# Two transformer layers on one NeuronCore: three of the memory's tiles are split into free columns beside the last projection

## Chip, cores and metric

The kernel runs on one core of a Trainium2 chip (trn2). The metric is the device time in microseconds (us) of one launch, the median of the runs shown. The engines are PE (TensorE), DVE (VectorE), ACT (ScalarE) and POOL (GpSimd). SP (SyncE) issues the transfers of the weights.

## The reference, cut to what matters

`reference()` is one hybrid layer (attention, a state-space mixer, a recurrent mixer, a feed-forward part), and then two layers of a second kind. Sequence 512, width 1024, fp32. Each of the two layers does:

```python
for l in range(2):
    y = swiglu_2(rms_norm(x, ffn1_pre_g[l]), ...);      x = x + 0.5 * rms_norm(y, ffn1_post_g[l])
    y = hybrid_mixer(rms_norm(x, mix_pre_g[l]), w_in[l], ...);  x = x + rms_norm(y, mix_post_g[l])
    y = memory_xattn(rms_norm(x, xa_pre_g[l]), rms_norm(mem, xa_mem_g[l]), wq, wk, wv, wo)
    x = x + rms_norm(y, xa_post_g[l])
    y = swiglu_2(rms_norm(x, ffn2_pre_g[l]), ...);      x = x + 0.5 * rms_norm(y, ffn2_post_g[l])

def memory_xattn(h, m, wq, wk, wv, wo):      # m: 256 x 1024
    q, k, v = h @ wq, m @ wk, m @ wv         # keys and values of the memory
    ...                                      # softmax attention of 4 heads of 256, then @ wo
```

`hybrid_mixer` projects its input to queries, keys and values of a sparse attention (96 units of scores, softmax and values here), and to the queries, keys, values and gate of a retention. The memory's keys and values do not depend on `x`, so the kernel makes them inside the mixer (class `MixerTwo`).

## The kernel before, in words

**Precision.** Every large product is made of three fp32r matmuls: high x high, high x low, low x high (`mm3`, L265). So each operand is split in two: ACT makes the high part (an activation that writes fp32r), DVE or POOL makes the low part (value minus high part). Weights come in chunks of two halves (128x1024 each): SP loads a half into one of four `raw` slots once the low part of the half before in that slot is made (`weight_load`, L231), ACT makes its high part (`weight_hi`, L238), POOL its low part (`weight_lo`, L250), in the mixer in four pieces. ACT and POOL work two chunks ahead of PE.

**The mixer's middle** is written as parallel streams, one for each engine. `Attention.pe` (L1323) runs 98 steps. In step s PE does the scores of units s and s+1 (even steps only), the transposes of unit s-1 (they wait for ACT's exp of it), the values product of unit s-2 (it waits for ACT's copy), and then takes two items ("beats") of a filler. DVE in step s adds the distances to the scores and takes the maximum (L1401, L1405), ACT takes the exp (L1373) and copies the transposes (L1382), and each then takes two beats of its own filler. So beat n belongs to step n // 2 on every engine. After each six units DVE finishes a group (L2704 to L2709), which waits for the group's last values product. Units of a group alternate between two compressed ones (32 keys) and four wide ones (384 keys in steps 48 to 71, 512 after).

**PE's filler** (`pe_filler`, L2545), one beat being six matmuls of 256 columns or three of 512: four chunks `rch` (64 beats), `vrch` and `grch` (two chunks of 16 beats each; `grch` is the last projection, the retention's gate, beats 96 to 127), three empty beats (128 to 130), the first chunk of the memory's keys `mkch[0]` (beats 131 to 138, `pe_first_keys`, one tile of the memory a beat for both column groups), `mkch[1:]` (24 beats), and four chunks of values `mvch` (32 beats, to beat 194). All of these chunks from `rch` on use PSUM banks 6 and 7, in turn. A chunk's group waits until the last reader of its bank is done (`ch.free`): for `mkch[0]` these are the gate's last two reads by DVE (L1486, `gr_used[6]` and `gr_used[7]`; each multiplies what ACT's tanh, L1475, left in `tmp` by the bank), for `mkch[1]` they are the evacuations of `mkch[0]` by DVE (L2796, `mk_kept[0]` and `mk_kept[1]`).

**The memory's split.** `self.mem` (8 tiles of 256 columns) lies in the columns where the memory's values will stand. Its split goes to `xa_mhi` and `xa_mlo`, which take the place of the mixer's input (`hhi`, `hlo`). That input is read by `grch` to its end, so ACT waits for the last matmul of `grch` (L2670) and then makes one tile a beat (L2672, beats 128 to 135; at tiles 3 and 5 it also makes a half of the weights of `mkch[1]`). DVE makes the low parts one beat later each (L2788, beats 129 to 136), waits two beats, and evacuates `mkch[0]` in beat 139. ACT has the silu's last tanh in beat 128 as well, and DVE the product after it: their generators give their four beats first and do the work at the start of the next one.

**Other streams beside the filler** are the squares of the memory, three norms, and the retention (from beat 98, every fourth beat; `Retention`, L2844), in each engine. They count the same beats, whatever the filler does in them. After the attention's last step PE begins the mixer's output projection: the half of chunk c0 that needs the retention only (`pe_out_half`, 24 matmuls of 512 columns), then the same half of c1. The weights of c1 are split after the attention on ACT and POOL: ACT waits for DVE's last group, squares (L2653), and then makes them (`weight_hi`, L2623).

Of the kernel before, what the change touches and what calls it, by code (L numbers as in the profile page):

```python
# [6 lines left out]
F32 = mybir.dt.float32  # L7
F32R = mybir.dt.float32r
ACT = mybir.ActivationFunctionType
ALU = mybir.AluOpType  # L10
AX_X = mybir.AxisListType.X

P = 128
# [251 lines left out]
def mm3(k, out, l, r, start, stop):  # L265
    t = k.nc.tensor
    t.matmul(out, l[0], r[0], start=start, stop=False)  # L267
    t.matmul(out, l[0], r[1], start=False, stop=False)  # L268
    return t.matmul(out, l[1], r[0], start=False, stop=stop)  # L269
# [26 lines left out]
def pe_stationary(k, ch, part, nk, k0=0, ktot=None, width=T, ready=None):  # L296


    t, ktot = k.nc.tensor, ktot or nk
    for m, b in enumerate(ch.banks):  # L300
        if ch.free[m] is not None:
            t.wait_ge(*ch.free[m])
        for kk in range(nk):
            if m == 0:
                pe_half_begin(k, ch, kk)
                if ready is not None:
                    for mark in ready(k0 + kk):
                        t.wait_ge(*mark)
            last = mm3(k, k.bank[b][:, 0:width], ch.weights(kk, m * P, P), part(k0 + kk), k0 + kk == 0, k0 + kk == ktot - 1)
            pe_step_end(ch, last, kk, kk == nk - 1, m == len(ch.banks) - 1)  # L310
            if width == T or kk % 2:
                yield
# [64 lines left out]
def beats(n):  # L377
    for _ in range(n):
        yield
# [25 lines left out]
class SquaresOfX:  # L405
# [9 lines left out]
    def tile(self, n):  # L415
        return self.place[:, n * T:(n + 1) * T]
# [1091 lines left out]
def idle_act(k, ch, steps):  # L1508
    yield from beats(steps)
    weight_hi(k, ch.c + 2)  # L1510
# [825 lines left out]
class MixerTwo:  # L2336
# [4 lines left out]
    def __init__(self, k, l, h):  # L2341
# [77 lines left out]

        self.mhi, self.mlo = alias("xa_mhi", k.at_h, F32R), alias("xa_mlo", k.at_h + 4 * T * 4, F32R)  # L2420
        self.m_hi, self.m_lo = k.marks("mem_hi", KT), k.marks("mem_lo", KT)
        self.mk_kept, self.mv_kept = k.marks("mem_keys", 8), k.marks("mem_values", 8)
        self.mkch = [Chunk(k, [6, 7], [self.mk_kept[2 * c], self.mk_kept[2 * c + 1]]) for c in range(4)]
        self.mvch = [Chunk(k, [6, 7], [self.mv_kept[2 * c], self.mv_kept[2 * c + 1]]) for c in range(4)]
# [120 lines left out]
    def pe_filler(self, h, part):  # L2545
        k = self.k
        for ch in self.rch:
            yield from pe_stationary(k, ch, part, KT)
        for ch in self.vrch + self.grch:
            yield from pe_moving(k, ch, h, 0, 256)  # L2550
        yield from beats(3)
        m = [self.mhi, self.mlo]
        tile = lambda n: [a[:, n * MEM:(n + 1) * MEM] for a in m]
        yield from self.pe_first_keys(self.mkch[0], tile)
        for ch in self.mkch[1:]:
            yield from pe_stationary(k, ch, tile, KT, width=MEM)
        for ch in self.mvch:
            yield from pe_moving(k, ch, m, 0, 256, width=MEM)

    def pe_first_keys(self, ch, tile):  # L2560

        k, t = self.k, self.k.nc.tensor
        for kk in range(KT):
            pe_half_begin(k, ch, kk)
            t.wait_ge(*self.m_lo[kk])
            for m, b in enumerate(ch.banks):
                if kk == 0 and ch.free[m] is not None:
                    t.wait_ge(*ch.free[m])
                last = mm3(k, k.bank[b][:, 0:MEM], ch.weights(kk, m * P, P), tile(kk), kk == 0, kk == KT - 1)
                pe_step_end(ch, last, kk, kk == KT - 1, m == 1)  # L2570
            yield

# [89 lines left out]
    def act_filler(self):  # L2662
        k, a = self.k, self.k.nc.scalar
        for c, ch in enumerate(self.rch):
            yield from idle_act(k, ch, 16)
        for c, ch in enumerate(self.vrch):
            yield from keep_tokens_act(k, ch, lambda tb: self.vr[:, tb * 512 + c * 256:tb * 512 + c * 256 + 256], self.vr_kept, root=k.r_tok)
        for c, ch in enumerate(self.grch):
            yield from silu_tokens_act(k, ch, self.gr_used, self.gr_tanh, k.tmp[0], c, k.r_tok_half, then=c == 0)
        a.wait_ge(*self.grch[-1].done[-1])  # L2670
        for n in range(KT):
            a.activation(self.mhi[:, n * MEM:(n + 1) * MEM], self.mem[:, n * MEM:(n + 1) * MEM], ACT.Copy, scale=k.p2(self.l, "xa_mem_g", n)).then_inc(self.m_hi.sem)  # L2672
            if n in (3, 5):
                weight_hi(k, self.grch[1].c + 2, n // 2 - 1)
            yield
        yield from idle_act(k, self.mkch[0], 3)
        for ch in self.mkch[1:]:
            yield from idle_act(k, ch, 8)
        for c, ch in enumerate(self.mvch):
            yield from keep_tokens_act(k, ch, lambda tb: self.mem_v[:, tb * D + c * 256:tb * D + (c + 1) * 256], self.mv_kept, root=self.m_rs, then=c < 3)  # L2680
# [94 lines left out]
    def dve_filler(self):  # L2775
        k, v = self.k, self.k.nc.vector
        for c, ch in enumerate(self.rch):
            dst, scale = ((self.qr, 1.0), (self.kr, 128.0 ** -0.5))[c // 2]
            yield from keep_dve(k, ch, lambda m: dst[:, (2 * (c % 2) + m) * T:(2 * (c % 2) + m + 1) * T], scale, self.r_kept)
        for ch in self.vrch:  # L2780
            yield from idle_dve(k, ch, 16)
        for c, ch in enumerate(self.grch):
            yield from silu_tokens_dve(k, ch, self.gr_used, self.gr_tanh, k.tmp[0], self.gr, c)
        yield
        for n in range(KT):
            o = slice(n * MEM, (n + 1) * MEM)
            v.wait_ge(*self.m_hi[n])
            v.scalar_tensor_tensor(self.mlo[:, o], self.mem[:, o], k.p2(self.l, "xa_mem_g", n), self.mhi[:, o].bitcast(F32), ALU.mult, ALU.subtract).then_inc(self.m_lo.sem)  # L2788
            yield
        yield from beats(2)  # L2790
        v.wait_ge(*self.m_row[0])
        for c, ch in enumerate(self.mkch):
            for m, b in enumerate(ch.banks):
                yield from beats(KT // 2 if c > 0 else 0)
                v.wait_ge(*ch.done[m])
                v.tensor_tensor(self.mem_k[:, (2 * c + m) * MEM:(2 * c + m + 1) * MEM], k.bank[b][:, 0:MEM], self.m_rows_of, ALU.mult).then_inc(self.mk_kept.sem)  # L2796
        for ch in self.mvch:
            yield from idle_dve(k, ch, 8)
# [28 lines left out]
    def pool_filler(self):  # L2827
        k = self.k
        for ch in self.rch + self.vrch + self.grch:
            yield from idle_pool(k, ch, 16)  # L2830
        yield from beats(3)
        for ch in self.mkch + self.mvch[0:3]:
            yield from idle_pool(k, ch, 8)
        yield from beats(8)
# [605 lines left out]
```

## Time and profile before

| | |
|---|---|
| time, three runs | 3268.32, 3270.23, 3270.97 us (median 3270.23) |
| profiled execution, its own time | 3270.5 us |
| its span (first to last instruction) | 3269.2 us |
| PE busy with matmuls | 3197.1 us, 98% of the span, 17820 matmuls |
| DVE, ACT, POOL busy | 40%, 38%, 41% |
| chain that ended last | PE 90%, DVE 3%, ACT 2%, POOL 2% |
| mean granted clock of TensorE | 0.998 of full speed |

How to read it: PE is the engine that bounds the kernel nearly everywhere. A share of 98% says that at most some 2% of the span can be won by filling PE's idle time, and each piece of it stands between two named instructions in the timeline. A matmul's duration in the profile holds the time in which it drains; the start of the next one tells the rate.

### The profile page before, as it was taken

To read this page: it belongs to the slowest core of one execution; us is meant where nothing else is said; L and a number is where in the kernel's file an instruction comes from. 1 tells how busy PE (TensorE), PEld (TensorE's weight loads), DVE (VectorE), ACT (ScalarE), POOL (GpSimd) and SP (SyncE) were. 2 spreads that over 40 slices of the span, in tenths; PEclk is the share of its full clock that TensorE was granted. 3 is DMA by queue.
4 is the path that set the end of the run, shared out by engine and by line. 5 is a ranking of instruction groups with operands and counts; after the bars stand their busy time and mean duration, and the time that the engine had idled before them with its cause. 6 is when DMAs were issued, how large, how long until landed. Compare 5 with 4: busy or idle time off the path is not lost.

```text
span 3269.2 us, 45423 instructions
## 1 busy us (share of the span) xinstructions
PE 3197.1 (98%) x17820; PEld 2724.0 (83%) x17820; DVE 1295.5 (40%) x2528; ACT 1233.6 (38%) x2305; POOL 1338.5 (41%) x867
## 2 busy tenths in 40 slices
PE   7999999999999999999999999999999999999998
PEld 6887788888888988888788889888987889798887
DVE  6474543215330434645353304331144564353311
ACT  4454332223232344554433223322344554433321
POOL 3452344453444432344334444444532244244443
PEclk9999999999999999999999999999999999999999
DMA  4221233332323241122223332333331123123232
GB/s 144 78 72 52 78 97 97 103 110 65 103 87 107 79 130 53 53 84 84 78 73 96 95 99 85 99 101 97 110 118 53 46 85 91 42 88 104 91 99 69
DMA packets 80948, 285.39 MB, mean 87 GB/s; under 512 B 8929, under 2 KB 11361, under 8 KB 80353
## 3 DMA queue, kind: packets, MB, share of 16 engines
q1 hardware_dynamic: 79728, 278.65, 27.9%
q10 hardware_dynamic: 1008, 3.84, 0.3%
q8 instruction: 143, 2.34, 0.3%
q14 instruction: 69, 0.56, 0.1%
HBM read 280.36 MB, written 2.10 MB: 86 GB/s over the span
## 4 chain that ended last, share of the span: by engine, by line
PE 90%; DVE 3%; ACT 2%; POOL 2%; issue 1%; DMA 1%; ACTq 0%; DVEq 0%; POOLq 0%
PE bank L267 23%; PE bank L269 22%; PE bank L268 22%; PE bank L275 4%; PE bank L276 4%; PE bank L277 4%; PE bank L1358 2%; POOL wlo L261 2%; PE bank L1334 2%; PE bank L1345 2%; PE bank L3107 1%; ACT whi L247 1%; PE bank L665 1%; DVE stat L1405 1%; DVE att_s L1401 0%
## 5 line engine op out<-in xcount | busy, mean ns | idle before, releaser
L261 POOL TENSOR_TENSOR wlo<-raw,whi 128x1024 fp32r<-128x1024 f32 (+2 forms) x776 | 1216.5, 1583 | 1580.6 <-ACT whi L247 1545.5
L267 PE MATMUL bank<-hhi,whi 128*128 128x512 f32 x2080 | 827.1, 398 | 5.5 <-DVE hlo L492 4.3
L268 PE MATMUL bank<-hlo,whi 128*128 128x512 f32 x2110 | 823.3, 390 | 0.0
L269 PE MATMUL bank<-hhi,wlo 128*128 128x512 f32 x2080 | 812.3, 391 | 0.0
L247 ACT ACTIVATE whi<-raw 128x1024 fp32r<-128x1024 f32 (+2 forms) x502 | 499.0, 1030 | 330.9 <-PE bank L269 267.1
L267 PEld LDWEIGHTS bank<-hhi,whi 128*128 128x128 f32 x2080 | 391.9, 188 | 86.4 <-issue 8.8
L268 PEld LDWEIGHTS bank<-hlo,whi 128*128 128x128 f32 x2110 | 397.7, 188 | 78.9 <-issue 1.0
L269 PEld LDWEIGHTS bank<-hhi,wlo 128*128 128x128 f32 x2080 | 391.4, 188 | 83.0
L267 PE MATMUL bank<-ff_ahi,whi 128*128 128x512 f32 x660 | 256.7, 389 | 0.0
L269 PE MATMUL bank<-ff_ahi,wlo 128*128 128x512 f32 x660 | 256.7, 389 | 0.0
L268 PE MATMUL bank<-ff_alo,whi 128*128 128x512 f32 x630 | 245.1, 389 | 0.0
L1242 ACT ACTIVATE ff_ahi<-tmp 128x512 fp32r<-128x512 f32 x110 | 69.6, 633 | 437.6 <-DVE tmp L1265 437.6
L624 DVE TENSOR_TENSOR tmp<-tmp,tmp 128x512 f32<-128x512 f32 x45 | 46.1, 1025 | 431.0 <-ACT tmp L646 430.7
L1255 DVE TENSOR_TENSOR tmp<-bank,row 128x512 f32<-128x512 f32 x110 | 75.1, 690 | 341.5 <-PE bank L269 312.3
L1373 ACT ACTIVATE att_s<-att_s,stat 128x32 f32<-128x32 f32 (+4 forms) x224 | 110.1, 492 | 262.6 <-DVE stat L1405 262.0
L1236 ACT ACTIVATE tmp<-tmp 128x512 f32<-128x512 f32 x110 | 68.6, 630 | 301.8 <-DVE tmp L1255 301.8
L1263 DVE TENSOR_TENSOR tmp<-bank,row 128x512 f32<-128x512 f32 x110 | 75.9, 690 | 222.4 <-PE bank L269 222.4
L267 PEld LDWEIGHTS bank<-ff_ahi,whi 128*128 128x128 f32 x660 | 123.9, 188 | 25.8
L269 PEld LDWEIGHTS bank<-ff_ahi,wlo 128*128 128x128 f32 x660 | 123.9, 188 | 25.7
L268 PEld LDWEIGHTS bank<-ff_alo,whi 128*128 128x128 f32 x630 | 118.3, 188 | 24.5
L267 PE MATMUL bank<-whi,hhi 128*128 128x256 f32 (+1 forms) x448 | 135.1, 302 | 2.2 <-POOL wlo L261 1.9
L1401 DVE SCALAR_TENSOR_TENSOR att_s<-consts,bank 128x32 f32<-128x32 f32 (+4 forms) x192 | 73.0, 380 | 155.3 <-PE bank L1334 154.7
(425 smaller groups left out, 5772.6 us busy)
## 6 DMA issues: line engine op xcount, KB each, us to landing
raw<-wstream SPq DMA_DIRECT2D x508, 512.0 KB, 3.5
raw<-wstream SPq DMA_DIRECT2D x20, 256.0 KB, 2.6
xa_v<-memT ACTq DMA_DIRECT2D x2, 1024.0 KB, 4.7
outT<-x SPq DMA_DIRECT2D x4, 512.0 KB, 2.8
raw<-wstream SPq DMA_DIRECT2D x4, 420.0 KB, 4.6
consts<-consts SPq DMA_DIRECT2D x1, 1062.0 KB, 13.6
x<-xT ACTq DMA_DIRECT2D x2, 512.0 KB, 8.5
x<-xT SPq DMA_DIRECT2D x2, 512.0 KB, 7.3
```

What stands on the lines that cost most here:

```text
L247: a.activation(h.hi[:, 0:h.cols], h.raw[:, 0:h.cols], ACT.Copy).then_inc(h.hi_made.sem)
L261: last = g.tensor_tensor(h.lo[:, o:o + step], h.raw[:, o:o + step], h.hi[:, o:o + step].bitcast(F32), ALU.subtract)
L267: t.matmul(out, l[0], r[0], start=start, stop=False)
L268: t.matmul(out, l[0], r[1], start=False, stop=False)
L269: return t.matmul(out, l[1], r[0], start=False, stop=stop)
L275: t.matmul(out, l[0], r[0], start=opens, stop=True, skip_group_check=True)
L276: t.matmul(out, l[0], r[1], start=False, stop=True, skip_group_check=True)
L277: return t.matmul(out, l[1], r[0], start=False, stop=True, skip_group_check=True)
L1255: v.tensor_tensor(k.tmp[m][:, :], k.bank[gate.banks[m]][:, :], k.row[:, :], ALU.mult).then_inc(self.normed.sem)
L1263: v.tensor_tensor(k.tmp[m][:, :], k.bank[up.banks[m]][:, :], k.row[:, :], ALU.mult).then_inc(self.up.sem)
L1373: a.activation(s[:, 0:n], s[:, 0:n], ACT.Exp, bias=k.stat[:, 80 + step % 4:81 + step % 4], accum_out=self.sums(g)[0][:, step % group:step ...
L1401: v.scalar_tensor_tensor(s[:, 0:n], u["dist"], u["slope"], k.bank[b][:, 0:n], ALU.mult, ALU.add).then_inc(self.biased.sem)
```

## The change

In columns 512 to 2047 of the memory's keys (`mem_k`, not yet written then) two places of 768 columns are made, `first_hi` and `first_lo`, for a second split of tiles 0, 1 and 2. ACT makes their high parts in beats 118, 121 and 124, DVE their low parts in beats 120, 123 and 126, both while `grch` still runs. PE's three empty beats go: `mkch[0]` starts at beat 128, with tiles 0, 1, 2 from the new place and tiles 3 to 7 from the old one. The split to the old place still makes all eight tiles (the later chunks read them), now in the order 3, 4, 5, 6, 7, 0, 1, 2, one a beat from beat 128 on ACT and 129 on DVE as before. `mkch[1]` starts at beat 136 and waits in its first group for the low parts of each tile. ACT loses two beats of idling after it (`weight_hi` of the chunks from `mkch[2]` on comes two beats earlier), DVE loses two (the first evacuation moves from beat 139 to 137), POOL two. PE's filler ends at beat 191 instead of 194.

```diff
@@ MixerTwo.__init__
+        at_first = self.at_mem + 2 * MEM * 4
+        self.first_hi, self.first_lo = (k.arena(at_first + n * 3 * MEM * 4, at_first + (n + 1) * 3 * MEM * 4)("xa_first", 3 * MEM, F32R) for n in range(2))
+        self.f_hi, self.f_lo = k.marks("mem_first_hi", 3), k.marks("mem_first_lo", 3)
@@ pe_filler
-        yield from beats(3)
         m = [self.mhi, self.mlo]
         tile = lambda n: [a[:, n * MEM:(n + 1) * MEM] for a in m]
         yield from self.pe_first_keys(self.mkch[0], tile)
-        for ch in self.mkch[1:]:
-            yield from pe_stationary(k, ch, tile, KT, width=MEM)
+        for c, ch in enumerate(self.mkch[1:]):
+            ready = (lambda n: [self.m_lo[self.LAST_TILES.index(n)]]) if c == 0 else None
+            yield from pe_stationary(k, ch, tile, KT, width=MEM, ready=ready)
...
+    LAST_TILES = (3, 4, 5, 6, 7, 0, 1, 2)
@@ pe_first_keys
-            t.wait_ge(*self.m_lo[kk])
+            if kk < 3:
+                t.wait_ge(*self.f_lo[kk])
+                part = [x[:, kk * MEM:(kk + 1) * MEM] for x in (self.first_hi, self.first_lo)]
+            else:
+                t.wait_ge(*self.m_lo[kk - 3])
+                part = tile(kk)
@@ act_filler
-            yield from silu_tokens_act(k, ch, self.gr_used, self.gr_tanh, k.tmp[0], c, k.r_tok_half, then=c == 0)
+            for n, _ in enumerate(silu_tokens_act(k, ch, self.gr_used, self.gr_tanh, k.tmp[0], c, k.r_tok_half, then=c == 0)):
+                if c == 1 and n in (6, 9, 12):
+                    o = slice((n - 6) // 3 * MEM, (n - 3) // 3 * MEM)
+                    a.activation(self.first_hi[:, o], self.mem[:, o], ACT.Copy, scale=k.p2(self.l, "xa_mem_g", (n - 6) // 3)).then_inc(self.f_hi.sem)
+                yield
         a.wait_ge(*self.grch[-1].done[-1])
-        for n in range(KT):
+        for i, n in enumerate(self.LAST_TILES):
...
-            if n in (3, 5):
-                weight_hi(k, self.grch[1].c + 2, n // 2 - 1)
+            if i in (3, 5):
+                weight_hi(k, self.grch[1].c + 2, i // 2 - 1)
             yield
-        yield from idle_act(k, self.mkch[0], 3)
+        yield from idle_act(k, self.mkch[0], 1)
@@ dve_filler
-            yield from silu_tokens_dve(k, ch, self.gr_used, self.gr_tanh, k.tmp[0], self.gr, c)
+            for n, _ in enumerate(silu_tokens_dve(k, ch, self.gr_used, self.gr_tanh, k.tmp[0], self.gr, c)):
+                if c == 1 and n in (8, 11, 14):
+                    i = (n - 8) // 3
+                    o = slice(i * MEM, (i + 1) * MEM)
+                    v.wait_ge(*self.f_hi[i])
+                    v.scalar_tensor_tensor(self.first_lo[:, o], self.mem[:, o], k.p2(self.l, "xa_mem_g", i), self.first_hi[:, o].bitcast(F32),
+                                           ALU.mult, ALU.subtract).then_inc(self.f_lo.sem)
+                yield
         yield
-        for n in range(KT):
+        for i, n in enumerate(self.LAST_TILES):
             o = slice(n * MEM, (n + 1) * MEM)
-            v.wait_ge(*self.m_hi[n])
+            v.wait_ge(*self.m_hi[i])
...
-        yield from beats(2)
         v.wait_ge(*self.m_row[0])
@@ pool_filler
-        yield from beats(3)
+        yield
```

## Rows read from the trace of the kernel before

**Rows 1.** Page of the kernel before, part 1: busy time of each engine.

```profile
PE 3197.1 (98%) x17820; PEld 2724.0 (83%) x17820; DVE 1295.5 (40%) x2528; ACT 1233.6 (38%) x2305; POOL 1338.5 (41%) x867
```

**Rows 2.** Waits of PE in the first layer of the pair, 1330 to 1360 us.

```profile
PE bank L1345 <- ACT att_s L1373: 3.2, 4, 1.3
PE bank L267 <- DVE xa_mlo L2788: 1.0, 1, 1.0
```

**Rows 3.** Timeline: start, us, engine, line, operation, [idle before <-releaser]; step 64 and transposes of 65.

```profile
1338.08 0.78 PE L1358 MATMUL bank<-m_v,att_p 128*128 128x64 f32 x6
...
1338.22 0.55 DVE L1401 SCALAR_TENSOR_TENSOR att_s<-consts,bank 128x384 f32<-128x384 f32 x1
...
1339.39 0.61 ACT L1373 ACTIVATE att_s<-att_s,stat 128x384 f32<-128x384 f32 x1 [2.46 <-DVE stat L1405]
...
1340.15 0.55 PE L1345 MATMUL bank<-consts,att_s 128*128 128x128 f32 x3 [1.29 <-ACT att_s L1373]
...
1340.38 0.46 ACT L1475 ACTIVATE tmp<-bank,stat 128x256 f32<-128x256 f32 x1
...
1340.87 0.42 DVE L1486 SCALAR_TENSOR_TENSOR m_gr<-tmp,bank 128x256 f32<-128x256 f32 x1 [1.51 <-ACT tmp L1475]
```

**Rows 4.** Timeline, the same layer, steps 67 to 69.

```profile
1347.19 0.33 PE L1345 MATMUL bank<-consts,att_s 128*128 128x128 f32 x1 [0.86 <-ACT att_s L1373]
...
1347.56 0.88 PE L1358 MATMUL bank<-m_v,att_p 128*128 128x64 f32 x6
...
1348.84 0.39 DVE L2704 TENSOR_TENSOR stat<-stat,m_gates 128x6 f32<-128x6 f32 x1
...
1351.30 0.33 PE L1358 MATMUL bank<-m_vc,att_p 128*128 128x64 f32 x2
...
1354.26 0.47 DVE L2788 SCALAR_TENSOR_TENSOR xa_mlo<-xa_v,par,xa_mhi 128x256 fp32r<-128x256 f32 x1
...
1355.14 0.55 PE L1345 MATMUL bank<-consts,att_s 128*128 128x128 f32 x3 [0.82 <-ACT att_s L1373]
...
1357.02 0.75 DVE L2796 TENSOR_TENSOR xa_k<-bank,tmp 128x256 f32<-128x256 f32 x2
```

**Rows 5.** The memory's tiles: DVE's split, its durations (ns least, median, most).

```profile
L2788 DVE SCALAR_TENSOR_TENSOR xa_mlo<-xa_v,par,xa_mhi x16: 474/486/682, 1341.3 to 2616.8; 128x256 fp32r<-128x256 f32 x16
```

**Rows 6.** Timeline of the second layer of the pair: transposes of step 69.

```profile
2617.72 0.55 PE L1345 MATMUL bank<-consts,att_s 128*128 128x128 f32 x3 [0.82 <-ACT att_s L1373]
```

**Rows 7.** Timeline: the end of the attention and the output projection's start.

```profile
1442.70 1.00 PE L1358 MATMUL bank<-m_v,att_p 128*128 128x64 f32 x8
...
1442.90 0.60 ACT L1382 ACTIVATE att_p<-bank 128x512 f32<-128x512 f32 x1 [0.68 <-PE bank L1345]
...
1445.04 1.00 PE L1358 MATMUL bank<-m_v,att_p 128*128 128x64 f32 x8
...
1446.64 0.40 PE L267 MATMUL bank<-m_rethi,whi 128*128 128x512 f32 x1
...
1449.25 7.65 POOL L261 TENSOR_TENSOR wlo<-raw,whi 128x1024 fp32r<-128x1024 f32 x3 [0.21 <-ACT whi L247]
...
1452.11 0.45 PE L267 MATMUL bank<-m_rethi,whi 128*128 128x512 f32 x1
```

**Rows 8.** Clock: timeline row, then windows (us, busy of each engine, PEclk, DMA share, GB/s).

```profile
1178.96 0.33 PE L1345 MATMUL bank<-consts,att_s 128*128 128x128 f32 x1 [1.94 <-ACT att_s L1373]
...
1177.00:1178.50 1.50, 0.02 (x1) 0.00 (x0) 0.00 (x0) 1.50 (x3) 1.50 (x1) 1.00 0.87 355
1178.50:1182.00 3.50, 3.04 (x11) 2.08 (x11) 0.00 (x0) 0.99 (x6) 3.21 (x3) 0.62 0.76 263
1182.00:1184.00 2.00, 2.00 (x12) 1.60 (x11) 1.06 (x4) 0.92 (x5) 2.00 (x1) 0.81 0.64 182
...
2441.50:2445.00 3.50, 3.43 (x13) 2.29 (x14) 0.24 (x1) 0.60 (x4) 3.21 (x3) 0.61 0.60 194
...
1338.00:1341.00 3.00, 1.71 (x16) 1.51 (x15) 1.45 (x5) 1.61 (x5) 0.00 (x0) 1.00 0.01 3
```

More of the change, by code:

```diff
@@ L2568, in pe_first_keys @@
                     t.wait_ge(*ch.free[m])
-                last = mm3(k, k.bank[b][:, 0:MEM], ch.weights(kk, m * P, P), tile(kk), kk == 0, kk == KT - 1)
+                last = mm3(k, k.bank[b][:, 0:MEM], ch.weights(kk, m * P, P), part, kk == 0, kk == KT - 1)
                 pe_step_end(ch, last, kk, kk == KT - 1, m == 1)
```

## The prediction

> **What bounds the kernel now.** The page comes first: PE is busy in 98% of the span [rows 1], so time is won or lost in PE's idle pieces alone. Second, PE's waits about the place of the change: five, 4.2 us in all, four of them for ACT's exp, one for a split of a memory tile [rows 2]. The timeline shows where. In step 64 PE ends the values product at 1338.86, has two empty beats, and stands until the transposes of unit 64 at 1340.15, because DVE reaches that unit at 1338.22, straight from earlier work, and ACT's exp ends at 1340.0 [rows 3]. Further waits come at the transposes of units 65 and 66 (0.86 us the latter), before the seventh memory tile, and at the transposes of unit 68 (0.82 us) [rows 4]. The second layer repeats it 1262.6 us later, wait by wait [rows 4, 6]. Third, the end of the attention, where the beats that are moved forward are missed [rows 7], and last the clock [rows 8].
>
> **The change, part by part**, for one layer.
>
> *The move.* Three beats of keys come to the place of three empty ones, and at the end three beats are missing. A beat costs 0.74 us: from 1442.70 to 1445.04 are a values product and two beats, from there to 1446.64 a product and one [rows 7], and the difference of 2.34 and 1.60 is the beat (a product is 0.86). Three beats are 2.22 us. A start that is late only because PE waited also loses some 0.16 us of drain: a matmul of 0.28 us is followed 0.12 us later when nothing waits.
>
> *Six splits more.* ACT's three stand in steps in which it waits for DVE before its exp: nothing; without that cover, 0.4 us each. DVE's take 0.49 us each [rows 5]. Those of beats 120 and 123 fall before it has to wait for scores: nothing. That of beat 126 does not: DVE comes to unit 64 without idle time [rows 3], so all that follows on DVE and ACT in step 64 is 0.49 us later. On SP nothing is added; weights of later chunks are split two beats earlier on ACT and POOL, while PE needs them three earlier, so their lead shrinks by one beat of eight: nothing, and if a piece were late, 0.74 us.
>
> *Bank 7, beat 128.* The first key tile goes to banks 6 and 7. Bank 6 is free. Bank 7 is read last by DVE's product of the gate (L1486), which needs ACT's tanh, which stands behind the exp of unit 64 and the copy of 63: it ends at 1341.29 [rows 3], now at 1341.78. Before, the three empty beats covered this. Now PE does the bank 6 half (0.37 us) until 1339.2 and stands **2.6 us**, with the transposes of unit 64 queued behind. They start at 1341.8 + 0.37 + 0.74 = 1342.9, 2.75 us later than now. The third beat makes it 3.5 us at the next scores. Then waits vanish: the scores of unit 65 are issued with those of 64, so DVE and ACT are not held up, and the waits at units 65 and 66 (0.19 and 0.86 us, with drain 1.4) and a short one behind them (0.2) go. At the values product of unit 65 PE is 1.9 us late: 1349.5 instead of 1347.56 [rows 4].
>
> *Bank 6, beat 136.* `mkch[1]` starts there and needs bank 6, which DVE empties in its beat 137, behind group finish, retention and the splits to the last tile. This chain now starts at the end of that product: 1350.4, not 1348.84, so 1.6 us later. The last split ends at 1354.26 + 0.47 + 1.6 = 1356.3, half of the evacuation pair (0.75 us) makes it 1356.7 [rows 4]. PE has ended the product of unit 66 by about 1353.6 (1351.30 + 0.33 + 1.9 to 2.0) and stands **3.1 us**. Two beats later, at 1358.2, come the transposes of unit 68, against 1355.14. So PE is 3.05 us later and 2.22 us of keys ahead: **0.8 us lost**. The order of the tiles (low parts of 0, 1 and 2 last) costs nothing beside it: they are made before the bank is free. That price is what the waits would be without it, 0.9 to 1.4 us, and is no addition.
>
> *The end.* ACT's copy ends at 1443.50, so the last values product follows the one before at once. The output projection's first half chunk takes 1452.11 - 1446.64 = 5.47 us. The low part that the second needs is ready at 1449.25 + 7.65/3 = 1451.80 [rows 7], 6.76 us after the last product starts, and its whole chain (group, squares, high part, low part) hangs on that product. PE is there after 0.86 + 5.47 = 6.33 us: **0.45 us lost** where the missing beat gave cover.
>
> *Sum without the clock:* 0.8 + 0.45 = 1.25 us a layer, 2.5 us for both. Its bounds: if both bank waits were covered, 2.22 - 0.45 = 1.8 us won a layer; if no later wait vanished, 1.4 more lost.
>
> *The clock.* PE waited 1.94 us at 1177.0, and soon after its resuming the granted clock fell to 0.62 in the mean of 3.5 us (the lower level, 1.2 GHz, for most of it), and the same at 2441.5; with the wait of 1.29 us it stayed at 2.4 GHz [rows 8]. No row shows a wait between the two in the mixers. The new ones are 2.6 and 3.1 us, nearer to 1.94 than to 1.29 and beyond it, so I expect a fall after each. Its price is the time not granted: 3.5 x 0.38 + 2.0 x 0.19 = 1.7 us [rows 8] where PE is dense, nothing where it stands anyway; both new waits are followed by dense work on which DVE's chain hangs. I take 1.5 us a fall, with 0 and 1.7 as ends. Four falls are 6.0 us. The Trainium skill (TensorE: Matmul & The Clock Gate, "What's actually happening") calls the throttled state the default and lets it return after an idle window; taken as wholly idle, that would not follow from waits like these, and its sum would be 2.5 us. The wait of 1.94 us in this trace speaks against that reading.
>
> *DVE beside POOL.* A split takes 0.47 us alone and up to 0.68 us [rows 5] beside POOL's pieces. The Trainium skill (SBUF — State Buffer, "SBUF: two separate sides") has the port pair of DVE and GpSimd as an exclusive lock that blocks the loser for a whole instruction. The row shows 0.2 us; a rival below has the rest.
>
> **Sum:** 3270.5 (the profiled execution's own time, 0.3 above the median of 3270.2) + 2.5 + 6.0 = 3279.0, or against the median **3278.7 us**. A measurement of this kernel tells 0.2%, 6.5 us: faster is below 3263.7, slower above 3276.8.
>
> **The rivals.**
> *Some falls fail to come.* Whether a wait brings the clock down may depend on where it lies. For it: only two instances, both of the same wait. Against: the new waits are longer. Three falls give 3277.2 (chance 0.10), two 3275.7 (0.12), one or none 3272.7 to 3274.2 (0.15).
> *The keys fill the idle time* (not slower): place, banks 6 and 7 at beats 128 and 136; price, 1.8 us won a layer and no fall, 3270.2 - 3.6 = 3266.6. It decides if the banks are free when PE arrives, within 0.1 us of 1338.9 and 1353.6. Against: the row of L1486 ends 2.4 us after the first. Chance 0.06.
> *Nothing comes of it*, since the filler is paced by two beats a step, and the three move to the end: 3270.2, chance 0.03.
> *DVE's chain is held by POOL:* with about three two-input splits between the group's finish and bank 6, each held a whole piece of some 0.7 us and not 0.2, that is 1.5 us more a layer: 3278.7 + 3.0 = 3281.7. It decides if POOL's pieces reach to 1356 in the new order; before, they stop at about 1353. Chance 0.06.
>
> **How the numbers follow.** The forecast with four falls has 0.48. Slower: 0.48 + 0.10 + 0.06 = 0.64. The rest but 0.01 is within 0.2%: 0.35. Faster by 6.5 us would need nearly all of 8.4 us of waits to go: 0.01. The range 3272.5 to 3281.5 holds the forecast and the cases of fewer falls, 0.85; the error of my two wait lengths (0.5 us each) lies in it.
>
> **What would show it.** Right: in the new profile the first key matmul at bank 7 waits about 2.6 us for DVE's L1486; the transposes of unit 64 start 2.75 us later; PE waits about 3.1 us in beat 136 for DVE's evacuation of the first keys; the second output chunk waits 0.4 to 0.5 us for POOL; stretches at half clock stand behind these waits in both layers. Wrong: a wait at bank 7 below 1.3 us, no wait at bank 6, or a mean clock at 0.998 still (four more falls of 3.4 us would make it about 0.996).

## The result, and the profile after

The changed kernel takes **3282.48 us** (median of 6 runs, 3280.48 to 3283.77) against 3270.23 us of six runs of the kernel before (3268.32 to 3270.97). The ratio is 1.0036, 95% interval 1.0026 to 1.0046: 12 us slower. The profiled execution took 3282.93 us, its span is 3281.6 us, its mean granted clock 0.995. The forecast was 3278.7 with a range up to 3281.5: the sign was right, the size too small by 4 us, and the time lies 1 us above the range.

First the page of the kernel after, part 1, against [rows 1]. PE is 6.5 us busier with the same 17820 matmuls, so part of the time lies inside the matmuls and not between them.

```profile
PE 3203.6 (98%) x17820; PEld 2728.3 (83%) x17820; DVE 1298.4 (40%) x2534; ACT 1234.7 (38%) x2311; POOL 1339.3 (41%) x867
```

Then PE's waits in the first layer, from 1330 to 1520 us (in all, times, longest, in us).

```profile
PE bank L1345 <- ACT att_s L1373: 3.5, 6, 1.0
PE bank L267 <- DVE xa_k L2817: 2.9, 1, 2.9
PE bank L267 <- DVE m_gr L1486: 2.5, 1, 2.5
PE bank L267 <- POOL wlo L261: 0.5, 1, 0.5
```

The timeline shows where. The two long ones are the expected waits for a bank: L1486 is DVE's last read of bank 7, L2817 the evacuation of the first keys (L2796 before). The rows that answer to [rows 3, 4]:

```profile
1338.40 0.36 PE L267 MATMUL bank<-xa_first,whi 128*128 128x256 f32 x1
...
1340.99 0.42 DVE L1486 SCALAR_TENSOR_TENSOR m_gr<-tmp,bank 128x256 f32<-128x256 f32 x1 [1.51 <-ACT tmp L1475]
...
1341.47 0.38 PE L267 MATMUL bank<-xa_first,whi 128*128 128x256 f32 x1 [2.47 <-DVE m_gr L1486]
...
1342.64 0.49 PE L1345 MATMUL bank<-consts,att_s 128*128 128x128 f32 x3
...
1348.89 0.27 PE L1345 MATMUL bank<-consts,att_s 128*128 128x128 f32 x1
...
1352.63 0.33 PE L1358 MATMUL bank<-m_vc,att_p 128*128 128x64 f32 x2
...
1355.44 0.75 DVE L2817 TENSOR_TENSOR xa_k<-bank,tmp 128x256 f32<-128x256 f32 x2
...
1355.92 0.39 PE L267 MATMUL bank<-xa_mhi,whi 128*128 128x256 f32 x1 [2.95 <-DVE xa_k L2817]
...
1357.98 0.84 PE L1345 MATMUL bank<-consts,att_s 128*128 128x128 f32 x3
...
1394.19 0.33 PE L1345 MATMUL bank<-consts,att_s 128*128 128x128 f32 x1 [1.01 <-ACT att_s L1373]
1394.67 1.10 PE L1358 MATMUL bank<-m_v,att_p 128*128 128x64 f32 x8 [0.15 <-ACT att_p L1382]
...
1410.81 0.66 PE L1345 MATMUL bank<-consts,att_s 128*128 128x128 f32 x4 [0.77 <-ACT att_s L1373]
```

The transposes of units 64, 66 and 68 start at 1342.64, 1348.89 and 1357.98. The layer itself starts 0.28 us earlier than before, so against the layer's own start they are 2.77, 1.98 and 3.12 us late. The waits of [rows 4] are gone. But two waits stand there that the prediction does not have: 1.01 us at the transposes of unit 78 (1394.19) and 0.77 us at those of unit 83 (1410.81). The second layer repeats all of them (2.47, 2.95, 1.02, 0.75 and 0.49 us).

The windows show the clock (busy time of each engine, PEclk, DMA share, GB/s), against [rows 8].

```profile
1341.50:1345.00 3.50, 3.50 (x30) 3.50 (x31) 1.78 (x4) 2.29 (x10) 0.00 (x0) 1.00 0.00 0
1356.00:1361.00 5.00, 5.00 (x30) 5.00 (x31) 4.31 (x8) 3.02 (x6) 3.79 (x6) 0.66 0.08 23
1582.00:1586.00 4.00, 4.00 (x7) 1.69 (x6) 0.68 (x1) 0.60 (x1) 0.00 (x0) 0.57 0.00 0
2625.00:2629.00 4.00, 3.72 (x22) 3.72 (x23) 3.93 (x8) 3.39 (x8) 2.57 (x4) 0.69 0.16 61
```

Behind the first new wait the clock stays at 2.4 GHz; behind the second it falls to 1.2 GHz for most of a stretch; and it falls at 1582, in the memory attention, whose code and waits (1.12 and 0.47 us) are those of before. The second layer does the same: none behind the first new wait, one behind the second (2625), one in the memory attention (2851). Below, a *fall* is such a stretch at 1.2 GHz; one of the usual length leaves 1.7 us not granted, a double one 3.4.

**One sum for two causes.** Each run lists its span and its mean clock, so (1 - clock) x span is the time that the clock did not grant. The clock is printed to 0.001, up to 1.6 us off in one run, so I use means over many runs (± is the standard error of the mean). The rest is what remains when that time is taken off.

| mean over the runs, us | time | not granted | rest |
|---|---|---|---|
| before (72 runs, beside all the kernels below) | 3270.7 | 8.8 | 3261.9 ± 0.2 |
| after (6 runs) | 3282.3 | 14.8 | 3267.6 ± 0.4 |

Some 4 us of the time not granted lie in every kernel behind the last matmul, where they cost nothing; they drop out of the differences. Window of the kernel before:

```profile
3265.00:3270.00 5.00, 0.00 (x0) 0.00 (x0) 0.46 (x2) 0.00 (x0) 0.00 (x0) 0.50 0.38 131
```

Two things on record bear the split out. Over the runs of one and the same kernel, a run that is longer by 1 us has 1.06 ± 0.06 us more not granted (14 sets of runs, 169 in all). And a kernel with 2.74 us of added matmuls (e6, below) has a rest that is 3.0 ± 0.3 us larger.

So of the 12 us some 6 are clock and **5.7 are the rest, that is, waits**, where the prediction had 6.0 and 2.5. The experiments ask what the other 3 us are, and whether the six belong to the two new waits of each layer.

### The profile page after: what moved, and what is told of

It reads as the page before. It is cut to its first block, busy times and chain, and to the rows that moved or that the text cites. A ratio compares the mean times of both kernels' runs of the same rounds, so it can differ in the third digit from the quotient of the medians.

```text
span 3281.6 us, 45437 instructions
## 1 busy us (share of the span) xinstructions
PE 3203.6 (98%) x17820; PEld 2728.3 (83%) x17820; DVE 1298.4 (40%) x2534; ACT 1234.7 (38%) x2311; POOL 1339.3 (41%) x867
## 4 chain that ended last, share of the span: by engine, by line
PE 89%; DVE 4%; POOL 2%; ACT 2%; issue 2%; DMA 0%; ACTq 0%; DVEq 0%; POOLq 0%
PE bank L267 23%; PE bank L268 22%; PE bank L269 22%; PE bank L275 4%; PE bank L276 4%; PE bank L277 4%; POOL wlo L261 2%; PE bank L1358 2%; PE bank L1334 2%; PE bank L1345 2%; PE bank L3128 1%; ACT whi L247 1%; PE bank L665 1%; DVE stat L1405 1%; DVE att_s L1401 1%
```

## The experiments

### Streams moved past others (e1, e2, e7)

In beat 153 instead of 155 POOL now starts eight pieces of weights. The timeline of the kernel after, DVE and POOL from 1386 to 1412, with the four subtractions of an earlier step ahead, when POOL is idle:

```profile
1336.76 0.87 DVE L2990 TENSOR_SCALAR m_qr<-m_qr,stat 128x128 f32<-128x128 f32 x4
...
1387.51 2.17 DVE L2974 SCALAR_TENSOR_TENSOR m_qr<-m_qr,stat,m_gr 128x128 f32<-128x128 f32 x4
...
1388.05 5.92 POOL L261 TENSOR_TENSOR wlo<-raw,whi 128x256 fp32r<-128x256 f32 x8 [7.04 <-ACT whi L247]
...
1391.03 2.35 DVE L2990 TENSOR_SCALAR m_qr<-m_qr,stat 128x128 f32<-128x128 f32 x4
1393.30 0.17 DVE L1401 SCALAR_TENSOR_TENSOR att_s<-consts,bank 128x32 f32<-128x32 f32 x1
...
1401.79 5.77 POOL L261 TENSOR_TENSOR wlo<-raw,whi 128x256 fp32r<-128x256 f32 x8 [7.82 <-ACT whi L247]
1407.52 0.56 POOL L2844 TENSOR_TENSOR stat<-stat,consts 128x1 f32<-128x1 f32 x1
...
1408.11 0.49 DVE L2787 TENSOR_SCALAR m_otok<-m_otok,stat 128x512 f32<-128x512 f32 x1 [2.65 <-POOL stat L2844]
```

The same work in the timeline of the kernel before:

```profile
1383.36 1.14 DVE L2953 SCALAR_TENSOR_TENSOR m_qr<-m_qr,stat,m_gr 128x128 f32<-128x128 f32 x4
...
1385.34 2.40 DVE L2969 TENSOR_SCALAR m_qr<-m_qr,stat 128x128 f32<-128x128 f32 x4
...
1385.55 5.76 POOL L261 TENSOR_TENSOR wlo<-raw,whi 128x256 fp32r<-128x256 f32 x8 [7.43 <-ACT whi L247]
...
1394.59 0.55 POOL L2823 TENSOR_TENSOR stat<-stat,consts 128x1 f32<-128x1 f32 x1 [3.29 <-DVE stat L2768]
...
1398.19 6.04 POOL L261 TENSOR_TENSOR wlo<-raw,whi 128x256 fp32r<-128x256 f32 x8 [1.18 <-ACT whi L247]
```

Before, POOL started behind the retention's four gate products (1.14 us) and slowed only the four subtractions (2.40 us; alone they take 0.87). After, its pieces meet both (2.17 and 2.35), and DVE comes to unit 78 at 1393.30, too late. Eight beats on, before, POOL took the norm's root first and then the weights; after, the weights (1401.79, 5.77 us) stand ahead of the root, and DVE waits 2.65 us for it with the scores of unit 83 behind it in its queue. Two theories: these two places are what is missing in my sum, or they are harmless.

**e1** gives POOL its two beats back, nothing else:

```diff
@@ pool_filler
-        yield
+        yield from beats(3)
```

> The changed kernel with one edit: POOL's three empty beats are back, so the low parts of the weights from mkch[2] on are made at the beats of the kernel before. Theory A (POOL moved past the other streams): the new waits at the transposes of units 78 (1.0 us, with its follow-up 1.5) and 83 (0.77, with drain 0.9) vanish, 2.4 us a layer, 4.8 us in all: about 3277.7, give or take a clock fall of 1.7. Theory B (those waits come from PE and ACT being late or from ACT's weights): both stay, within 1 us of 3282.5.

Measured: 3279.04 us, ratio 1.0024 (1.0015 to 1.0034); 12.8 us not granted, rest 3266.0 ± 0.2. Each theory was right about one wait. The second is gone. The first stays, because POOL's start there is set by ACT's `weight_hi`, which still comes two beats early. PE's waits on L1345 in the timeline of e1 from 1390 to 1420, with none at unit 83 (about 1408):

```profile
1392.61 0.33 PE L1345 MATMUL bank<-consts,att_s 128*128 128x128 f32 x1 [1.01 <-ACT att_s L1373]
...
1399.08 0.66 PE L1345 MATMUL bank<-consts,att_s 128*128 128x128 f32 x4 [0.43 <-ACT att_s L1373]
...
1417.66 0.66 PE L1345 MATMUL bank<-consts,att_s 128*128 128x128 f32 x4 [0.44 <-ACT att_s L1373]
```

**e2** gives ACT its two beats back as well (`idle_act(k, self.mkch[0], 3)`).

> As e1_pool_back, and ACT's two beats of idling after mkch[0] are back as well, so the high parts from mkch[2] on come as before the change. In e1 the wait at unit 83 was gone and that of 1.01 us at unit 78 was not: DVE's gate products (four) and centring (four) both ran beside POOL's pieces, 2.17 and 2.35 us, where before only the second did (1.14 and 2.40). Theory A (POOL starts when ACT's high part is there, so ACT's two beats decide): the gate products take 1.1 to 1.2 us again, the wait at unit 78 goes, 1.5 us a layer: 3 us under e1, about 3276. Theory B (PE's lateness is the cause): the 1.01 us stays, 3279.

Measured: 3280.66 us, ratio 1.0030 (1.0020 to 1.0040). Both waits are gone (POOL's pieces start at 1392.49 and the root stands ahead of the next ones), the waits of 2.48, 2.88 and 0.49 us stay. The gate products take what they took before, in the timeline of e2:

```profile
1390.31 1.14 DVE L2974 SCALAR_TENSOR_TENSOR m_qr<-m_qr,stat,m_gr 128x128 f32<-128x128 f32 x4
```

The time is 4.7 us above the 3276 of the theory whose waits came true, and alone would say that nothing was won. The clock explains it: means over the runs are 3280.3 with 16.8 us not granted, a rest of 3263.5 ± 0.4, **4.1 us below that of after**. The two waits with the 0.15 us beside them are 1.93 us a layer, 3.9 for both: the same number within the error.

**e7** gives ACT alone its beats back, to see whether the order in POOL's queue is the cause of the second wait.

> The changed kernel with ACT's two beats back, but POOL's not. Theory A (unit 78 hangs on when the high parts come, unit 83 on POOL's order: in beat 161 it takes the weights ahead of the norm's root): the wait at unit 78 goes; at unit 83 POOL now stands before the root until ACT's later high part, and the wait grows from 0.77 to 2.5 us or more. In sum -1.5 and +1.8 or more a layer: 3282 to 3286. Theory B (both are one cause): both waits go, 3278.

Measured: 3287.79 us, ratio 1.0056 (1.0039 to 1.0073), four runs only, the slowest of all and above the expected 3282 to 3286. The wait at unit 78 is gone, the other has grown. What is slower than after is clock: 20.5 us are not granted, and the rest, 3267.6 ± 0.7, is that of after. DVE and PE in the timeline of e7:

```profile
1407.50 0.49 DVE L2787 TENSOR_SCALAR m_otok<-m_otok,stat 128x512 f32<-128x512 f32 x1 [4.67 <-POOL stat L2844]
...
1408.73 0.41 PE L1334 MATMUL bank<-m_kc,m_q 64*128 64x32 f32 x4 [1.65 <-DVE att_s L1401]
1410.20 1.12 PE L1345 MATMUL bank<-consts,att_s 128*128 128x128 f32 x4 [1.06 <-ACT att_s L1373]
```

Behind these two stands a double fall, in the window of e7:

```profile
1410.00:1417.00 7.00, 6.80 (x33) 6.80 (x33) 1.43 (x9) 2.53 (x10) 0.00 (x0) 0.51 0.00 0
```

POOL's weights still stand ahead of the root in its queue, and now wait there for ACT: DVE stands 4.67 us instead of 2.65. So each wait has its own cause: unit 78 is ACT's two beats (when POOL's pieces start), unit 83 is POOL's two (the order of its queue).

### The splits alone (e3)

All four engines keep the beats of before; only the early splits and the order of the tiles stay:

```diff
@@ pe_filler, act_filler, dve_filler, pool_filler (against the kernel after)
+        yield from beats(3)
-        yield from idle_act(k, self.mkch[0], 1)
+        yield from idle_act(k, self.mkch[0], 3)
+        yield from beats(2)
-        yield
+        yield from beats(3)
```

> The changed kernel with PE's, ACT's, DVE's and POOL's beats all as before; the six early splits a layer stay, and PE takes tiles 0 to 2 from the first places. Theory A (waits for the banks, not the splits, are the cost): one DVE split of 0.49 us before unit 64 shows, 0.3 to 0.5 us a layer: 3270.5 to 3271.5. Theory B (the added work on DVE and ACT is the cost): 3275 or more.

Measured: 3271.70 us, ratio 1.0004 (0.9995 to 1.0014); 10.5 us not granted, rest 3261.2 ± 0.6. Six more splits a layer cost nothing that can be measured. The waits change places: 1.69 and 2.02 us at units 64 and 68 instead of 1.29 and 0.82, while the wait of 0.95 for a split is gone.

### Bank 6 first (e4)

Tiles 0 to 2 go to bank 6 alone in beats 128 and 129, to bank 7 in beats 130 and 131, so that DVE has time to read bank 7:

```diff
@@ pe_first_keys (cut; first(m, kk, ...) does the three matmuls of tile kk into bank 6 + m)
...
+        for kk in range(3):
+            t.wait_ge(*self.f_lo[kk])
+            first(0, kk, early(kk), kk == 0)
+            if kk > 0:
+                yield
+        for kk in range(3):
+            first(1, kk, early(kk), kk == 0)
+            if kk == 1:
+                yield
...
```

> The changed kernel, but PE's first keys go to bank 6 for tiles 0, 1, 2 (beats 128 and 129) and to bank 7 for them only in beats 130 and 131. Theory A (the wait at bank 7 holds the transposes of unit 64): that wait of 2.5 us goes to under 0.5, the transposes of unit 64 come 0.5 us later than before the change and not 2.8; but the second wait, for bank 6, is then bound by DVE's own work and grows to 3.0 to 3.3 us, so only some 0.7 us a layer is won: about 3281. Theory B (the first wait is the price and the second follows from it): 2 us or more a layer, 3278 or less.

Measured: 3279.93 us, ratio 1.0027 (1.0016 to 1.0038). The wait for bank 7 is gone, PE stands 0.57 us at unit 64; but it stands 3.48 us for bank 6 in beat 136 and is behind it at a mean clock of 0.56 for 7 us (a double fall; in the second layer, behind the same wait, a single one). Timeline row and window of e4:

```profile
1355.37 0.58 PE L267 MATMUL bank<-xa_mhi,whi 128*128 128x256 f32 x1 [3.48 <-DVE xa_k L2828]
```

```profile
1355.30:1362.30 7.00, 6.93 (x36) 6.93 (x37) 4.45 (x9) 3.17 (x7) 5.64 (x8) 0.56 0.37 126
```

14.5 us are not granted, the rest is 3265.5 ± 0.4, 2.1 less than after. Of two waits that are bound by one queue (DVE's), removing the first lengthens the second.

### Whose are the falls of the clock (e6, and both kernels again)

A fall had appeared in the memory attention, whose code is unchanged. Was it the shift in time? e6 is the kernel before with six redundant matmuls of 512 columns (1.37 us) a layer at the output projection's start:

```diff
@@ pe_out_half
+                for _ in range(2 if half == 0 and m == 0 and kk == 0 and b == self.out.chunks[0][4].banks[0] and ch is self.out.chunks[0][4] else 0):
+                    mm3(k, k.bank[b][:, :], ch.weights(kk, m * P, P), self.cat(kk), True, True)
```

> The kernel before the change, with six redundant matmuls of 512 columns (1.37 us) a layer ahead of the output projection's first half chunk, and nothing else changed. It shifts the memory attention by 1.4 us in the first layer. Theory A (whether the clock falls at that stage's waits depends on when they come): the granted clock falls in the memory attention of at least one layer, 1.6 us each: 3270.2 + 2.7 + 1.6 to 3.2 = 3274.5 to 3276.1. Theory B (the fall belongs to the changed mixers): no new fall, 3272.9.

Measured: 3274.03 us, ratio 1.0009 (1.0000 to 1.0019), between the two theories; 8.8 us not granted, as before, rest 3264.9 ± 0.3. No fall in the memory attention and none at 1178; new ones at 340, behind the waits of 1.24 and 0.58 us at 2523, and behind that of 1.28 us at 2606. One profile of a shifted kernel cannot tell a shift from chance. So both kernels were profiled once more, unchanged:

> The kernel before, unchanged, in one more profiled execution. Theory (falls of the clock are a draw among the same waits): the number or the place of the stretches at half clock differs from the first profile of it (one in each memory attention's first wait of 1.94 us, 7.3 us of clock not granted in all), while every wait between the same two instructions keeps its length within 0.1 us. Rival (each wait brings its own fall, always): the same places, 7.3 us again. The span less the clock not granted should be 3262 +- 1 us either way.

> The changed kernel, unchanged, in one more profiled execution. Theory (a draw): the waits at the keys of 2.5 and 3.0 us stay, but the falls behind them are not the same set as in the first profile (behind the second and none behind the first, 15.2 us not granted in all). Rival (fixed by the code): the same places and 15 us. The span less the clock not granted should be 3266 to 3268 us either way.

They took 3273.91 and 3282.41 us. (The wait of 1.94 us, which the expectation puts in the memory attention, stands in the mixer's attention, L1345.) Of the waits of 0.5 us and more from 1120 us on nearly every one kept its length within 0.1 us. Those that did not mostly stand behind a fall: in the kernel before the wait of 0.86 us at unit 66 is gone behind the fall at 1341, in that after the wait for bank 6 in the second layer is 2.52 and not 2.95 behind a double fall; a wait for POOL at 2428 is 0.89 and not 0.72. The falls were others. Windows of the second execution of the kernel before:

```profile
1258.00:1262.00 4.00, 3.38 (x24) 3.23 (x25) 1.34 (x7) 2.18 (x9) 0.00 (x0) 0.84 0.30 118
1341.50:1346.00 4.50, 4.48 (x25) 4.20 (x25) 3.26 (x7) 3.29 (x11) 0.00 (x0) 0.62 0.01 2
1575.00:1580.00 5.00, 3.11 (x10) 1.36 (x9) 1.82 (x6) 1.61 (x5) 0.00 (x0) 0.81 0.00 0
1580.00:1585.00 5.00, 5.00 (x15) 2.71 (x14) 1.38 (x2) 1.20 (x2) 0.00 (x0) 0.85 0.00 0
```

and of the kernel after:

```profile
1178.50:1182.00 3.50, 3.25 (x18) 2.46 (x19) 1.01 (x4) 1.22 (x8) 3.21 (x3) 1.00 0.69 246
1340.00:1347.00 7.00, 6.95 (x46) 6.77 (x47) 3.21 (x9) 4.33 (x15) 1.38 (x2) 0.76 0.00 0
1356.00:1363.00 7.00, 6.99 (x38) 7.00 (x39) 4.39 (x8) 3.11 (x6) 5.71 (x8) 0.59 0.24 74
2608.50:2615.50 7.00, 6.92 (x37) 6.92 (x37) 2.17 (x6) 4.46 (x15) 0.48 (x1) 0.58 0.00 1
2625.00:2632.00 7.00, 6.74 (x34) 6.74 (x34) 4.64 (x9) 3.37 (x8) 5.45 (x8) 0.54 0.29 99
```

In the kernel before the clock now also fell behind the wait of 1.29 us of [rows 3], behind one of 1.26 with one of 0.59, and at 1578 in the memory attention: that fall needs neither the changed mixer nor a shift. In the kernel after it stayed up behind the wait of 1.94 at 1178 and in the memory attention, and fell behind both new waits, twice as long behind the second, in the second layer behind both. So the same wait brings a fall in one execution and none in another.

One profile tells little; the fourteen profiles of this text together tell more. Counted over all of them, both layers:

| wait of PE, us | where | falls |
|---|---|---|
| 1.94 | mixer's attention, first layer | 5 of 14 |
| 1.94 | the same in the second layer | 12 of 14 |
| 1.12 and 0.47 | memory attention | 13 of 28, in the unchanged kernel before 1 of 4 |
| 2.02 | unit 68 in e3 and e12 | 1 of 4 |
| 2.5 | bank 7 | 4 of 12, two of them double |
| 2.5 to 3.1 | bank 6; unit 68 in e8 | 12 of 12, four of them double |
| 3.5 | bank 6 in e4; unit 68 in e9 and e10 | 6 of 6, five double |

So the 17 waits from 2.88 us on, and the 2.52 us behind a double fall, brought the clock down every time. Below that the length does not order the odds: 1.94 us brought it down more often than 2.5.

### Idle time given back elsewhere (e8, e9, e10)

If filler at step 64 is worth something, the end should not pay for it. **e8** keeps the keys at beat 128 but puts the three empty beats between the first and the second chunk of keys, the other engines as before from there on:

```diff
@@ pe_filler (cut; idle_act, DVE's beats(2) and POOL's beats(3) are those of e3)
+        yield from beats(3)
         for c, ch in enumerate(self.mkch[1:]):
...
```

> The three empty beats of PE stand between mkch[0] and mkch[1] and not ahead of mkch[0]; ACT, DVE and POOL have their beats from mkch[1] on as before the change. So the wait at bank 7 (beat 128) stays and those at bank 6 and at the end cannot be. Theory A: wait at bank 7 of 2.5 us; DVE's chain to unit 68 comes 1.3 to 1.6 us later than before, and nothing is won for it: 3270.5 + 2.6 to 3.2, and a clock fall of 1.7 us a layer if PE then stands over 3 us in step 68: 3273.5 to 3277. Theory B (the bank 7 wait is paid back by the waits that go): within 1 us of 3270.5.

Measured: 3277.01 us, ratio 1.0018 (1.0008 to 1.0027), 13.8 us not granted, rest 3262.7 ± 0.4. The waits are 2.47 us for bank 7 and 3.10 us at unit 68 (2.96 in the second layer), now for ACT's exp. **e9** adds e4's order.

> As e8_gap3, with the order of e4_bank6_first. Theory A: no wait for a bank is left; unit 64 waits 0.5 us for its exp, and all follows DVE's own chain, 0.3 to 0.5 us a layer later than before (the DVE split ahead of unit 64): 3271 to 3271.5, plus up to 1.7 us a layer if the wait of over 3 us in step 68, now in one piece, brings the clock down: up to 3275. Theory B (moving the keys early frees PE and wins by itself): under 3270.

Measured: 3275.99 us, ratio 1.0017 (1.0008 to 1.0027), 1 us above what was expected at most. The rest is 3260.2 ± 0.3, **1.7 below before**: this is what the moved keys are worth in this order with the clock left out. But 16.0 us are not granted: most of the idle time that lay in five pieces before is gathered in one wait, with a double fall behind it in both layers. **e10** takes two empty beats instead of three.

> Bank 6 first for tiles 0 to 2, and two empty beats between the first and the second chunk of keys, ACT, DVE and POOL keeping the same distance to PE. Against the same order with three empty beats (3276.0 us): theory (DVE's chain sets unit 68's exp, PE's empty beats are only taken from its wait there) the transposes of unit 68 start at the same time, PE waits somewhat longer in all before them, one beat less is missing at the end, so 3276 +- 1.5 us. Rival (the streams behind POOL and ACT now come one beat early and the waits of units 78 and 83 come back in part): 3277 to 3279.

Measured: 3276.13 us, ratio 1.0015 (1.0006 to 1.0024). The same wait (3.48 us), the end wait of 0.50 us back: the beat taken out brings nothing. The rest is 3261.4 ± 0.3, 1.2 us above e9 (the end waits are 1.0), with 14.6 us not granted.

### Two splits moved behind the scores (e12)

In e9 DVE goes from the group's finish through retention and two splits (beats 134 and 135) to the scores of unit 68. e12 puts DVE's two idle beats ahead of the last three splits:

```diff
@@ dve_filler (against e9)
-            yield
-        yield from beats(2)
+            yield from beats(3 if i == 4 else 1)
```

> Bank 6 first and three empty beats as before, and DVE's two idle beats stand ahead of the last three splits instead of behind them (beats 136 to 138 instead of 134 to 136; PE reads those tiles from beat 139). Two splits of 0.6 us leave DVE's queue ahead of unit 68's scores. Theory (PE's wait of 3.49 us at unit 68 is DVE's queue, and its length is what doubles the stretch at half clock behind it): the wait falls to about 2.3 us, the stretch of 6.8 us becomes one of 3.4 or none, so 1.2 us a layer without the clock and up to 1.7 more with it: 3276.0 - 2.4 to - 5.8 = 3270.2 to 3273.6. Rival (ACT or the group's finish sets unit 68's exp, not the splits): the wait stays above 3 us and the time at 3276. Second rival: the wait only moves to unit 69's transposes: 3275 to 3276.

Measured: **3270.43 us**, ratio 0.9997 (0.9989 to 1.0006), 5.6 us below e9. Unit 68 in the timeline, first of e9 and then of e12:

```profile
1354.20 0.90 PE L1345 MATMUL bank<-consts,att_s 128*128 128x128 f32 x3 [3.49 <-ACT att_s L1373]
```

```profile
1354.05 0.65 PE L1345 MATMUL bank<-consts,att_s 128*128 128x128 f32 x3 [2.03 <-ACT att_s L1373]
```

and the windows of e12 behind it, in the first layer and in the second:

```profile
1354.00:1357.50 3.50, 3.45 (x18) 3.45 (x19) 3.40 (x11) 1.24 (x4) 0.17 (x1) 0.55 0.52 152
2621.00:2625.00 4.00, 4.00 (x30) 3.32 (x31) 2.36 (x6) 3.46 (x8) 2.44 (x4) 1.00 0.01 2
```

The wait shrank by 1.46 us; the fall behind it is now a single one in the first layer, and fails to come in the second behind the same wait. Means: 11.6 us not granted (16.0 in e9), rest 3258.9 ± 0.5. The larger part of the 5.6 us is clock; of the wait that went, 2.9 us in both layers, only 1.3 ± 0.5 shows in the rest, in part because a wait of 0.59 us for bank 6 comes in the second layer; the remainder is not explained. Against the kernel before the rest is 3.0 us better and the clock 2.8 us worse, so the two are equal, and no kernel run here beats the one before.

## Why the prediction was right or wrong

**Right, by its own steps.** The wait for bank 7 (2.6 forecast, 2.47 measured) and unit 64 late by 2.77 us (2.75); the vanished waits at units 65 and 66 (unit 66 late by 1.98, forecast 1.9 to 2.0); the wait for bank 6 (3.1, 2.95) and unit 68 late by 3.12 us (3.05); the end (0.45, 0.49). e2, which has these steps alone, stands 1.6 us above the kernel before without the clock, where I had 2.5. The six splits cost nothing in the time, though the wait at unit 64 grew by 0.4 us (e3). The sign was right.

**Failed: "weights of later chunks are split two beats earlier on ACT and POOL ... nothing".** I compared the moved work with PE's need for it (eight beats of lead) and not with what it is moved past. It cost 3.9 us in waits, 4.1 ± 0.6 in the rest (after against e2): some 2.6 by DVE running beside POOL's pieces (e1 against e2) and 1.5 by the order of POOL's queue (after against e1). The rival "DVE's chain is held by POOL" had the mechanism and nearly the size (3.0 us), but named the stretch up to bank 6; it struck ten steps later, at unit 78.

**Right in sum by luck, wrong in mechanism: a fall behind each new wait, 1.5 us each.** The means give 6.0 us. But I read a threshold out of three instances of before (fall at 1.94 us, none at 1.29), and between these two there is none: the same wait of 1.29 us had a fall in another execution, that of 1.94 had none in yet another, and the new wait of 2.47 us had none in the first profile. In the five profiles that have both new waits (after twice, e1, e2, e7) the wait for bank 6 had a fall 10 times of 10 and that for bank 7 only 3 of 10. Four of these 13 were double, so that the two together make 17 lengths of 1.7 us, 5.8 us a profile (an estimate from these counts). Too few falls at one wait and too long ones at both cancelled. The Trainium skill (TensorE: Matmul & The Clock Gate, "What's actually happening") also calls the number of slow matmuls at a kernel's start variable from run to run. The two executions of each kernel show the same in the middle of one, with falls in different places, and I had left that out. With 1.6 + 4.1 + 6.0 in place of 2.5 + 0 + 6.0 the sum is 3281.9 us, against 3282.48 measured; the terms are taken from the means of the same runs, so this is book-keeping and no second test.

**What stays open.** How the odds depend on what stands in and around a wait was not settled: the same wait of 1.94 us had 5 falls of 14 in one layer and 12 in the other. Nor is it known why 16.8 us are not granted in e2 and 12.8 in e1, which has the same waits and one more. Nor was a version tried that shortens the wait of 2.03 us in e12 further.

## What to carry to other kernels

When filler moves in a kernel of in-order streams, list for each engine which instructions of other streams it is moved past, its own queue's order first, and only then its distance to the consumer. Idle time that is bound by another engine's queue does not go away by filling it: it comes back behind the filler, and in one piece it costs more than in five, because the clock falls more surely and for longer (16.0 us not granted in e9, 8.8 in the kernel before); take work out of the queue that binds (e12) instead. And compare such kernels by means over many runs with the time not granted taken apart: e2 against after is 1.8 us by the medians and 4.1 us without the clock.

## What the runs showed of the hardware

- The same program with the same waits had its stretches at 1.2 GHz in different places in two executions. In the mixers they were seen behind waits from 1.24 to 3.5 us, and failed to come behind waits of 1.94, 2.03 and 2.47 us; behind the 17 waits from 2.88 to 3.5 us they never failed to. A stretch that is twice as long was seen behind waits of 2.47 us and more, and once behind two waits of 1.65 and 1.06 us close together (e7).
- DVE beside POOL's 256-column pieces (0.74 us each): four gate products of 128x128 with two inputs in SBUF take 2.17 us and not 1.14, four subtractions with one input 2.35 and not 0.87. The Trainium skill (SBUF — State Buffer, "SBUF: two separate sides") lets a DVE instruction that needs the ports shared with POOL wait for a whole instruction of POOL's, here 0.74 us; the rows show 0.26 and 0.37 us more for each on average. Why it is less than a piece was not looked into. The instruction with one input is hit no less.
